# Two feed-forward layers in Strassen form: down-projection steps reordered, and the last normalisation's offset handled without accumulating transfers

## What is computed

```
def swiglu(u, wg, wu, wd):
    return (jax.nn.silu(u @ wg) * (u @ wu)) @ wd          # wg, wu: 1024 x 2816, wd: 2816 x 1024
# every sub-layer:
# x <- LayerNorm(alpha * x + w * (1 + gate(c)) * f(x * (1 + scale(c)) + shift(c)))   alpha = 2 ** 0.25
```

## Time and profile before

| what | value |
|---|---|
| median of 3 runs | 2316.21 us |
| profiled execution, its own time | 2313.89 us |
| its span | 2312.1 us |
| TensorE busy | 2142.1 us (93%) |
| VectorE busy | 1481.0 us (64%) |
| ScalarE busy | 997.7 us (43%) |
| GpSimd busy | 604.8 us (26%) |
| mean granted TensorE clock | 0.967 |
| DMA, FFN 2's end (last five of 40 slices) | 248, 294, 268, 273, 73 GB/s |

### The profile page before, as it was taken

One profiled execution on the slowest core, in us unless ns is written; L12 is line 12 of the kernel. 1 busy time (PEld: TensorE's weight loads), 2 busy tenths in 40 slices (PEclk: granted clock), 3 DMA queues, 4 the chain that ended last, 5 costly groups with the idle time before them and its releaser, 6 DMA issues. The chain is left out here.

```text
span 2312.1 us, 29054 instructions
## 1 busy us (share of the span) xinstructions
PE 2142.1 (93%) x10377; PEld 1778.8 (77%) x10377; DVE 1481.0 (64%) x2298; ACT 997.7 (43%) x1891; POOL 604.8 (26%) x630
## 2 busy tenths in 40 slices
PE   6999999999997999799998899898999999998697
PEld 5888888877885887787886788776888888876485
DVE  6777777745876414787887577734755445446489
ACT  3433333334435112877876466613633333333243
POOL 0366666423000000132212000001244444413110
PEclk9999999999996999799999999998999999999798
DMA  7354444489831311300000000122222222279993
GB/s 258 114 169 165 164 164 164 155 266 286 266 88 47 128 46 33 95 1 1 1 1 1 1 1 1 65 91 93 81 82 82 82 82 82 87 248 294 268 273 73
DMA packets 201507, 265.97 MB, mean 115 GB/s; under 512 B 19024, under 2 KB 117392, under 8 KB 201367
## 3 DMA queue, kind: packets, MB, share of 16 engines
q1 hardware_dynamic: 178904, 205.42, 26.2%
q0 software_dynamic: 22464, 58.73, 10.6%
HBM read 224.25 MB, written 37.76 MB: 113 GB/s over the span
## 5 line engine op out<-in xcount | busy, mean ns | idle before, releaser
L2604 ACT ACTIVATE nsaa_exps<-nsaa_scores,nsaa_neg_max 128x64 f32<-128x64 f32 (+8 forms) x192 | 108.0, 577 | 16.1 <-DVE nsaa_neg_max L2635 15.6
L1268 DVE SCALAR_TENSOR_TENSOR late_part_late<-ada_rows,far_silu_c,late_part_late 128x1024 f32<-128x1024 f32 x56 | 108.5, 1937 | 2.3 <-DMA ada_rows<-in_w_ada 2.2
L2635 DVE TENSOR_REDUCE nsaa_neg_max<-nsaa_scores 128x1 f32<-128x640 f32 (+8 forms) x104 | 90.3, 871 | 28.7 <-PE nsaa_scores L2560 28.1
L2650 DVE TENSOR_TENSOR nsaa_turned_lo<-nsaa_ring,nsaa_turned_hi 128x512 fp32r<-128x512 f32 (+1 forms) x148 | 97.6, 685 | 15.2 <-ACT nsaa_turned_hi L2613 13.8
L1957 PE MATMUL in_acc<-in_w_hi,mix_in_u_hi 128*128 128x494 f32 x256 | 99.4, 388 | 7.3 <-DVE in_w_lo L1920 7.3
L580 ACT ACTIVATE ffn1A_t_hi<-ffn1A_t 128x512 fp32r<-128x512 f32 x80 | 48.5, 629 | 130.4 <-POOL ffn1A_t L573 97.2
L580 ACT ACTIVATE ffn2A_t_hi<-ffn2A_t 128x512 fp32r<-128x512 f32 x80 | 48.5, 629 | 124.3 <-POOL ffn2A_t L573 88.2
L759 DVE TENSOR_TENSOR ffn2A_u<-ffn2A_u,ffn_banks 128x512 f32<-128x512 f32 x40 | 27.5, 688 | 114.6 <-PE ffn_banks L703 110.5
L1957 PE MATMUL in_acc<-in_w_lo,mix_in_u_hi 128*128 128x494 f32 x256 | 99.2, 387 | 0.0
L1957 PE MATMUL in_acc<-in_w_hi,mix_in_u_lo 128*128 128x494 f32 x256 | 99.0, 387 | 0.0
L2613 ACT ACTIVATE nsaa_turned_hi<-nsaa_ring 128x512 fp32r<-128x512 f32 (+1 forms) x148 | 84.2, 600 | 26.8 <-PE nsaa_ring L2572 24.5
(11 more groups left out here) (599 smaller groups left out, 6877.7 us busy)
## 6 DMA issues: line engine op xcount, KB each, us to landing
ada_rows<-in_w_ada POOLq DMA_DIRECT2D x56, 512.0 KB, 4.7
ffn_raw_g<-in_ffn_wg SPq DMA_DIRECT2D x44, 512.0 KB, 3.8
ffn_raw_u<-in_ffn_wu SPq DMA_DIRECT2D x44, 512.0 KB, 4.9
ffn1R_pair<-hidden POOLq DMA_DIRECT2D x33, 256.0 KB, 8.3
ffn2R_pair<-hidden POOLq DMA_DIRECT2D x33, 256.0 KB, 8.3
early_w<-in_w_ada SPq DMA_DIRECT2D x16, 512.0 KB, 7.0
mix_in_w_raw<-in_w_in SPq DMA_DIRECT2D x32, 247.0 KB, 2.6
ffn_rest<-in_ffn_wd SPq DMA_DIRECT2D x27, 256.0 KB, 12.9
```

What stands on the lines that cost most here:

```text
L1268: dve.scalar_tensor_tensor(out=part_late[:, v, :], in0=ada[:, n % 2, :], scalar=silu_c[:, k:k + 1], in1=part_late[:, v, :], op0=ALU.mult, ...
L2604: made = act.activation(exps[n % slots][:, r, 0:u.widths[r]], scores[:, m % 2, u.columns(r)], ACT.Exp, bias=neg_max[:, n % SUMS, r:r + 1], ...
L2635: top = dve.reduce_max(at, rows, AX, negate=True)
L2650: dve.tensor_tensor(turned_lo[0:u.keys, j % copies, cols], bank[0:u.keys, cols], turned_hi[0:u.keys, j % copies, cols].bitcast(F32), ALU.s ...
```

## The change

- **Order of the steps.** P1 and P7 use the same hidden and weight quarters, so they are interleaved: P1's first three steps, then P7 and P1 in turn, then P5, P6, P4, P2, P3 (`STEP`, `AT`). VectorE makes three blends per P7 step (`blend`): P7's weight sum, P7's hidden sum (before, an accumulating transfer), and P5's weight sum from P1's weights (before, loaded again). P5 needs no slot at all. `fill_last` and the separate `b12` loads go. Per FFN and pair there are 11 plain transfers and 3 accumulating ones where there were 13 and 4.
- The combination follows the order: a new result C22 = U2 + P7 is made on VectorE from two kept tiles; three products are kept by ScalarE instead of two; P4's gate product is separate (before, it was folded into `take`). P4 and P3 are split in two halves of 512.
- x comes back in eight consecutive steps (22 to 29), paced by `PACE`, and is grown in steps 26 to 33.
- **FFN 2.** The offset row is added by a second VectorE instruction per tile instead of an accumulating transfer. The offset row is not written over the output first; instead GpSimd adds it to tiles 0 to 3, and multiplies and adds for tiles 4 and 5 (`SHARED`), eight [128, 1024] instructions, before plain stores. `last_steps` takes five steps instead of four.
- The sign of one half of h changes places in the gate phases (one instruction each, same count).

```
-P1, P5, P6, P2, P3, P7, P4 = range(7)
-QUAD = (0, 1, 0, 1, 1, 0, 0)
-JOINS = (False, False, True, False, False, True, True)
-STEPS = 7 * PAIRS
+P1, P7, P5, P6, P4, P2, P3 = range(7)
+QUAD = (0, 1, 1, 0, 0, 1, 1)
+JOINS = (False, False, False, True, True, False, False)
+
+
+LAG = 3
+STEP = [(P1, j) for j in range(LAG)]
+for j in range(PAIRS):
+    STEP += [(P7, j)] + [(P1, j + LAG)] * (j + LAG < PAIRS)
+STEP += [(p, j) for p in (P5, P6, P4, P2, P3) for j in range(PAIRS)]
+AT = {step: n for n, step in enumerate(STEP)}
+STEPS = len(STEP)
 RING, SLOTS, LANES = 5, 7, 4
-LAST_STEPS = range(STEPS - 4, STEPS)
-
-COPY_AT, BACK_AT, GROW_AT, PAIR_AT, LAST_PAIR_AT = 3, 22, 22, 8, 50
-LAST_AT = (61, 64, 67, 70)
+LAST_STEPS = range(STEPS - RING, STEPS)
+
+SPLITS = tuple(2 if p in (P4, P3) else 1 for p, _ in STEP)
+
+COPY_AT, PACE = 4, 7
+BACK_FROM, GROW_FROM, ROWS_AT = AT[P5, 0], AT[P5, 4], AT[P4, 0]
+LAST_AT = (AT[P2, 7], AT[P2, 10], AT[P3, 2], AT[P3, 5])
...
+def slot_no(n):
+
+    return n if n < AT[P5, 0] else n - PAIRS
...
+def blends_done(p, j):
+
+    return {P7: 3 * j + 2, P5: 3 * j + 3, P6: 3 * PAIRS + j + 1, P4: 4 * PAIRS + j + 1}[p]
+
+
+SHARED = 6
+
...
     def slot_vacant(self, sp, q):
 
-        p = q // PAIRS
-        if p in (P5, P6, P2):
-            sp.wait_ge(self.t_done, t_no(q))
-        if p in (P1, P2, P3, P7):
-            sp.wait_ge(self.d_split, cut_no(q))
+        p, j = step_of(q)
+        if p == P1:
+            sp.wait_ge(self.t_done, blends_done(P5, j))
+        if p in (P6, P4):
+            sp.wait_ge(self.t_done, blends_done(p, j))
+        if p != P6:
+            sp.wait_ge(self.d_split, cut_no(AT[p, j]))
 
     def fill(self, sp, n):
 
-        p, j = divmod(n, PAIRS)
+        p, j = STEP[n]
+        if p == P5:
+            return
         if n < 2:
             sp.wait_ge(self.t_made, 4 * (FC - 2))
             sp.wait_ge(self.split, split_all(FC - 1))
-        elif n >= SLOTS:
-            self.slot_vacant(sp, n - SLOTS)
-        h, w, done = self.slot(n)[:, 0:HALF], self.slot(n)[:, HALF:D], self.slot_in[n % SLOTS]
-        if p in (P1, P2, P7):
-            f = 2 * j + (p == P2)
-            if p == P1:
-                sp.wait_ge(self.h_out, 32 * (f + 1))
-            sp.dma_start(h, self.hidden_at(f, 0)).then_inc(done, 16)
-        f, e = {P1: (0, 0), P5: (0, 0), P6: (1, 1), P2: (1, 0), P3: (1, 1), P7: (1, 1)}[p]
+        elif slot_no(n) >= SLOTS:
+            self.slot_vacant(sp, slot_no(n) - SLOTS)
+        h, w, done = self.slot(n)[:, 0:HALF], self.slot(n)[:, HALF:D], self.slot_sem(n)
+        if p in (P1, P4, P2):
+            f, row = {P1: (0, 0), P4: (1, 1), P2: (1, 0)}[p]
+            sp.wait_ge(self.h_out, 32 * (2 * j + f + 1))
+            sp.dma_start(h, self.hidden_at(2 * j + f, row)).then_inc(done, 16)
+        f, e = {P1: (0, 0), P7: (1, 1), P6: (1, 1), P4: (1, 0), P2: (1, 0), P3: (1, 1)}[p]
         sp.dma_start(w, self.weight_at(2 * j + f, e)).then_inc(done, 16)
-        if p == P7:
-            if j >= LANES:
-                sp.wait_ge(self.t_done, t_no(n - LANES))
-            sp.dma_start(self.b12[:, j % LANES, :], self.weight_at(2 * j, 1)).then_inc(self.b12_in[j % LANES], 16)
+
+    def fill_ahead(self, sp, n):
+
+        if n >= LAG and (n - LAG) % 2 == 0 and (n - LAG) // 2 < PAIRS:
+            self.fill_pair(sp, (n - LAG) // 2)
+        self.fill(sp, n)
...
+    def blend(self, dve, n):
+
+
+        p, j = STEP[n]
+        if p not in (P7, P6, P4):
+            return
         t, w = self.pair[:, j, HALF:D], self.slot(n)[:, HALF:D]
         self.slot_landed(dve, n)
-        if p == P5:
+        if p == P7:
+            first = self.slot(AT[P1, j])
             dve.wait_ge(self.pair_in[j % LANES], 32 * (j // LANES + 1))
+            dve.tensor_tensor(w, w, t, ALU.subtract).then_inc(self.t_done, 1)
+            self.slot_landed(dve, AT[P1, j])
+            dve.tensor_tensor(self.slot(n)[:, 0:HALF], first[:, 0:HALF], self.pair[:, j, 0:HALF], ALU.add).then_inc(self.t_done, 1)
+            dve.wait_ge(self.t_done, 3 * j + 1)
+            dve.tensor_tensor(t, t, first[:, HALF:D], ALU.subtract).then_inc(self.t_done, 1)
+        elif p == P6:
+            dve.wait_ge(self.d_split, cut_no(AT[P5, j]))
             dve.tensor_tensor(t, t, w, ALU.subtract).then_inc(self.t_done, 1)
-        elif p == P6:
-            dve.wait_ge(self.d_split, cut_no(P5 * PAIRS + j))
-            dve.tensor_tensor(t, t, w, ALU.subtract).then_inc(self.t_done, 1)
-        elif p == P2:
-            dve.wait_ge(self.d_split, cut_no(P6 * PAIRS + j))
+        else:
+            dve.wait_ge(self.d_split, cut_no(AT[P6, j]))
             dve.scalar_tensor_tensor(out=t, in0=t, scalar=-1.0, in1=w, op0=ALU.mult, op1=ALU.subtract).then_inc(self.t_done, 1)
...
-        if p in (P6, P2):
-            pe.wait_ge(self.kept, 4 * (p - P6) + i + 1)
-        if p in (P3, P7, P4):
-            pe.wait_ge(self.taken, TAKEN[{P3: P2, P7: P6, P4: P7}[p]] + i + 1)
+        if p in (P5, P6, P2):
+            pe.wait_ge(self.kept, {P6: 0, P5: 4, P2: 8}[p] + i + 1)
+        if p in (P4, P3):
+            pe.wait_ge(self.taken, TAKEN[{P4: P6, P3: P2}[p]] + i + 1)
...
+        if p == C22:
+            dve.wait_ge(self.taken, TAKEN[P6] + i + 1)
+            dve.wait_ge(self.kept, 4 + i + 1)
+            dve.tensor_tensor(p5, u2, p7, ALU.add).then_inc(self.taken, 1)
+            return
...
     def down(self, dve, n):
 
         if n:
-            if (n + 2) // PAIRS in (P5, P6, P7):
-                self.blend_weight(dve, n + 2)
             self.split_step(dve, n)
-        if n // PAIRS == P2:
-            self.blend_weight(dve, n)
-        for p in (P6, P2, P3, P7):
-            first = (p + 1) * PAIRS + COPY_AT
+        if n == LAG - 1:
+            self.blend(dve, LAG)
+        if n + 2 > LAG and n + 2 < STEPS:
+            self.blend(dve, n + 2)
+        for p in (P6, P4, P2):
+            first = AT[p, PAIRS - 1] + COPY_AT
             if n == first:
                 for i in range(4):
                     self.take(dve, p, i)
             if p != P6 and first < n <= first + 4:
                 self.settle(dve, p, n - first - 1)
+            if p == P6 and n in range(first + 1, first + 9, 2):
+                i = (n - first) // 2
+                self.take(dve, C22, i)
+                self.settle(dve, C22, i)
...
-        for n in range(3):
+        for n in range(LAG):
             ffn.fill(sp, n)
-        ffn.store_hidden(sp, FC - 1)
         sp.wait_ge(ffn.made, made_all(FC - 1))
         sp.wait_ge(x_kept, 16 * TT)
-        for n in range(3, P4 * PAIRS):
-            ffn.fill(sp, n)
-            if n == PAIR_AT:
-                sp.wait_ge(ffn.h_out, 32 * FC)
-            if PAIR_AT <= n < PAIR_AT + PAIRS:
-                ffn.fill_pair(sp, n - PAIR_AT)
-            if n == BACK_AT - 2:
+        for n in range(LAG, STEPS):
+            ffn.fill_ahead(sp, n)
+            if n == LAG + 4:
+                ffn.store_hidden(sp, FC - 1)
+            if n == BACK_FROM - 4:
                 for rows, place in zip(norm_rows, (ffn.gain_rows, ffn.offset_rows)):
                     sp.dma_start(place[:, :], rows.to_broadcast([P, D])).then_inc(ffn.rows_in, 16)
-            if n in range(BACK_AT, BACK_AT + 2 * TT, 2):
-                i = (n - BACK_AT) // 2
+            if BACK_FROM <= n < BACK_FROM + TT:
+                i = n - BACK_FROM
+                sp.wait_ge(ffn.d_split, cut_no(n - PACE))
                 sp.dma_start(x_sb[:, i, :], x_rows[i * P:(i + 1) * P, :]).then_inc(ffn.x_back[i], 16)
-            if n == BACK_AT + 2 * TT:
-                sp.dma_start(g_row[:, :], out_rows[1][0].to_broadcast([P, D])).then_inc(out_in, 16)
-                sp.dma_start(b_row[:, :], out_rows[1][1].to_broadcast([P, D])).then_inc(out_in, 16)
-                sp.dma_start(out_dram[0, 0:T // 2, :], out_rows[1][1].to_broadcast([T // 2, D])).then_inc(based, 16)
-            if LAST_PAIR_AT <= n < LAST_PAIR_AT + PAIRS:
-                ffn.fill_last(sp, n - LAST_PAIR_AT)
-        for i in range(TT // 2, TT - 1):
-            sp.wait_ge(finished, i - TT // 2 + 1)
+            if n == ROWS_AT:
+                for row, place in zip(out_rows[1], (g_row, b_row)):
+                    sp.dma_start(place[:, :], row.to_broadcast([P, D])).then_inc(out_in, 16)
...
-        pool.wait_ge(offset_grown, 1)
-        for i in range(TT):
-            pool.wait_ge(grown_half, i + 1)
-            pool.dma_start(x_sb[:, i, :], ffn.offset_rows[:, :], accum_op=ALU.add).then_inc(ffn.grown, 16)
         for j in range(PAIRS):
...
+        pool.wait_ge(out_in, 32)
         for i in range(TT // 2):
             pool.wait_ge(scaled, i + 1)
-            pool.dma_start(out_dram[0, i * P:(i + 1) * P, :], x_sb[:, i, :], accum_op=ALU.add).then_inc(stored_first, 16)
+            pool.tensor_tensor(x_sb[:, i, :], x_sb[:, i, :], b_row[:, :], ALU.add).then_inc(shifted, 1)
+            pool.wait_ge(shifted, i + 1)
```

(29 more changed lines are left out.)

207 lines of the change are left out of this document (92 added, 115 removed).

## The result

The changed kernel takes 2300.2 us (median of four runs, 2299.3 to 2303.7), the kernel before in the same session 2315.4. The ratio is 0.9936, 95% interval 0.9922 to 0.9949: 15 us faster where I had predicted 29. The time lies inside the range of 2266 to 2306; the gain is half the forecast.

A forecast was written before the change was run, and what follows sets the result against it. The prediction took DMA engines to bound FFN 2 up to step 60 and VectorE the end. It summed 6.9 (FFN 1) + 34.2 (FFN 2) - 12.1 (end) = 29.0 us saved: 2313.89 to about 2285, range 2266 to 2306.

The forecast's parts named there:

- The 40 us starvation goes, and what remains late has to be latency, not volume.: FFN 2's down phase: transfer demand falls from 227 us to about 160, so the stretch at 2152 no longer starves.
- The hand-over from P6 to P4: P4 waits for a `take` behind the split four steps on: 3.4 us against 2.72, so 0.7 us lost.
- the order does not relieve the queues: Rival: x's tiles burst with P5's and P6's accumulations, so starvation only moves; half the gain gone, about 2302; chance 0.05.
- the 34 us: FFN 2's down phase to the end of step 60: 175.7 us against 209.9, 34.2 saved.
- The start and the loop: Interleaved stage: P7's first weights late, 1.4 us; slot loop of period 6.0 against 5.44 us, 3.3 us.
- rivals two and three: Landings of 5.5 us in interleaved stage, 2304.7, chance 0.13; slower, loop becomes bound, at 8 us 2334.7, chance 0.06.
- The last steps: Interleaved stage's end: `pair` 10 issued late, 2.4 us; in FFN 2 gain and offset rows ahead of `pair` 8, 1.5 us.
- The end: From step 60's end VectorE sets the time: 54.1 + 17.5 + 2.5 = 74.1 us against 62.0, 12.1 lost.
- The price per GpSimd instruction: At the end, VectorE waits 2.5 us for each of seven 1024-wide GpSimd instructions, 17.5 us.
- The fourth: The fourth of GpSimd's eight end instructions costs VectorE nothing: it falls beside half statistics, which read one operand.
- The first rival: GpSimd does not stand in VectorE's way at the end: 15.5 us less, 2269.4; chance 0.18.
- The sign I had named: At the end, VectorE's 1024-wide instructions take 2.5 to 3.7 us wherever L1508, L1513 or L1515 run.

The follow-up runs named there:

- x_vector: Kernel before, with FFN 2's offset row added to x's eight tiles by a second VectorE instruction, not accumulating transfers, in the old order: 2295.8 us, ratio 0.9911.
- gain_rows_late: Changed kernel with the last three `pair` tiles issued earlier and x's gain and offset rows behind step 21's fill instead of step 18's: 2289.9 us, ratio 0.9886.

## Why the prediction was half right

- **What bounds it.** Right: DMA engines up to step 60, VectorE behind it. The volume fell (38.0 and 11.8 MB now, against 45.4 and 17.8), and the queues' engine time with it, from 227 to 170 us (43.9% and 21.9% of 259); I had 160.
- **"The 40 us starvation goes, and what remains late has to be latency, not volume."** This step failed. It counted demand over the whole phase (160 us of engine time against 201) and not over the stretch in which it falls. In steps 33 to 44 P6's and P3's accumulations, the last rows and P4's loads come together at a share of 1.07. The hand-over from P6 to P4 was priced at 0.7 us for rounding, split, blend and take, as if the loads were there; it took 8.3, since the `take` stands behind the blends of steps up to 49 and their weights landed after 18 to 19 us. With either the sums or the rows moved it takes 1.0, close to the price. So of the 13.2 us missing in FFN 2, 7.6 are this term's and 5.9 those of the interleaved stage's last steps, below; the remaining terms came out 0.4 better than forecast. This is the rival "the order does not relieve the queues" in small: "the starvation of 2152 only moves there", to P4's start. The rival named the x tiles as the cause, and they were not: steps 22 to 35, where the tiles come back, lose 0.6 us, as predicted (0.5).
- **Which part pays.** The prediction gave the credit for the 34 us to the change as a whole. The runs put it mainly on x's offset: x_vector alone saves 21 us.
- **The interleaved stage.** The start and the loop together: 4.7 us predicted, 4.2 measured to step 15. The landings on the chain are 4.98, 3.19, 3.80, 4.00 and 3.46 us, 3.9 on average, where I had taken 3.85; rivals two and three fall. The last steps (`pair` 10 and half of the rows, 3.9 us) were right in place and mis-sized: 9.8 us. I had priced the queue by engine time (0.75 us per 256 KB); gain_rows_late shows 4.4 us for 1 MB of rows, for which I had taken 1.5. The stage took 73.8 us for its 22 steps where the sign I had named was 67.
- **FFN 1.** 6.9 us predicted, 5.1 in the profiled pair. Its loss is 10.2 to 14.5 us in the kernels with the same FFN 1 code as the changed one, and 15.6 and 14.5 in the two with the old: 0 to 5 us saved.
- **The end.** Direction and mechanism right; 12.1 lost predicted, 8.4 measured. VectorE's own work was right: 70.5 - 2.5 - 13.3 = 54.7 us against the 54.1 added up. The price per GpSimd instruction was too high. A GpSimd instruction that nothing holds up takes 2.4 us, and of it VectorE lost 2.0 to 2.2 where a two-input instruction met its start, less where a one-input or a PSUM one came first: 13.3 for the seven instead of 17.5. The fourth was free, for the reason given. The first rival, no interference, falls. The sign I had named was in part wrong: the stretched instructions are, but for a short one of 1.18 us, 512-wide splits, gate products and additions at 2.1 to 2.9 us, while VectorE's 1024-wide ones kept their 1.2 to 1.3.
- **The rest.** Of the 4.7 us between the two down phases 0.7 are the last tile's; 4.0 lie in code that the change does not touch, which varies as much between executions. That these went against the forecast in the profiled pair is chance. By terms: 29.0 - 1.8 - 4.7 - 13.2 + 3.7 = 13.0.

## What to carry to other kernels

Sum the transfers of every stretch of some ten steps, not of the phase, and set each load's lead beside what is queued ahead of it: at a share of 1.07 a landing of 14.9 us cost nothing here and one of 19 us cost 4 to 5. The lead itself shrinks when the queue that issues the loads is held up. Rows and sums that nobody needs for twenty steps are what to move, and moving one of several may be enough. Where VectorE sets the end, a 1024-wide two-input instruction handed to GpSimd cost it more (12.7 us for eight, 1.6 each, and up to 2.2) than doing the work itself (9.5 us, 1.2 each); an accumulating store added nothing to the end here. And undo the parts of a change one by one: here one edit of eight instructions was worth at least as much as all of it.

## What the runs showed of the hardware that was not expected

- A 512-wide VectorE instruction held up by GpSimd ends 0.55 us after it, whatever was left of GpSimd's when it came (2.89, 2.11 and 2.71 us for 0.69 alone). The 1024-wide split of the earlier trace rows ended 1.08 us after it: VectorE does all its work once GpSimd is through. And GpSimd itself is held up when VectorE was first (3.42 us instead of 2.36 behind a 1024-wide instruction, 2.7 to 2.8 behind 512-wide ones).
- At one place 16 us of accumulations and 3 us of plain rows (engine time) are worth the same: with either moved, 7.2 of 8.3 us of loss go.
- Code that does not differ takes 1344 to 1348 us between the two down phases, with a granted clock of 0.99 or 0.87 right after FFN 1.
